# Delta rule: the next head's decay products between the halves of the first doubling, its sums of squares in four parts ahead of turns 1 to 4

## The reference, cut to what matters

```python
def chunked_gated_delta(q, k, v, g, beta):
    b = jnp.cumsum(g, axis=-1)
    diff = b[..., :, None] - b[..., None, :]
    dec = jnp.where(incl, jnp.exp(jnp.where(incl, diff, 0.0)), 0.0)
    k_beta = k * beta[..., None]
    A = jnp.where(strict, jnp.einsum('nbhid,nbhjd->nbhij', k_beta, k) * dec, 0.0)
    lhs = A + jnp.eye(C, dtype=A.dtype)
    ...
    sol = lax.linalg.triangular_solve(lhs, rhs, left_side=True, lower=True, unit_diagonal=True)
    ...
def deltanet_branch(q, k, v, z, a, bgate, conv_w, a_log, dt_bias, norm_g):
    qkv = jax.nn.silu(depthwise_conv(jnp.concatenate([q, k, v], -1), conv_w))
    q = l2norm(q.reshape(B, L, DN_HEADS, DN_DK)) * (DN_DK ** -0.5)
    k = l2norm(k.reshape(B, L, DN_HEADS, DN_DK))
```

## Time and profile before

| | us |
|---|---|
| timed runs | 2511.9, 2514.2, 2514.21 (median 2514.2) |
| the profiled execution | 2511.17 |
| its span | 2509.4 |
| TensorE busy in the span | 2391.3 (95%), 14993 matmuls |
| VectorE busy | 1712.1 (68%) |
| ScalarE busy | 1020.1 (41%) |
| GpSimd busy | 946.7 (38%) |

### The profile page before, as it was taken

The page is one execution under the profiler, slowest core; times in us unless marked ns, Lnnn a source line. Parts: engine busy times, 40 slices in busy tenths (PEclk is TensorE's granted clock), DMA queues, the critical chain, the costliest instruction groups (busy, mean ns, idle before and its releaser), DMA issues. The chain is left out here.

```text
span 2509.4 us, 44836 instructions
## 1 busy us (share of the span) xinstructions
PE 2391.3 (95%) x14993; PEld 1448.8 (58%) x14993; DVE 1712.1 (68%) x3600; ACT 1020.1 (41%) x1767; POOL 946.7 (38%) x612
## 2 busy tenths in 40 slices
PE   7999998989999999988999999998999999999998
PEld 6444444458878888875465556564656544444443
DVE  7535432037777677763260778998999689998887
ACT  4322332224433344322322344335989634443331
POOL 4421422412331223311522477876767422222220
PEclk9999999999999999999999999999999999999999
DMA  5321322221110011002323378987999699999994
GB/s 205 107 68 34 101 67 70 71 74 35 34 33 8 25 33 33 8 0 68 101 85 118 119 265 283 306 297 250 358 380 396 211 381 389 389 389 368 349 357 155
DMA packets 174318, 440.40 MB, mean 175 GB/s; under 512 B 17408, under 2 KB 83584, under 8 KB 174096
## 3 DMA queue, kind: packets, MB, share of 16 engines
q1 hardware_dynamic: 132752, 288.20, 33.3%
q0 software_dynamic: 36864, 134.23, 14.9%
q10 hardware_dynamic: 4608, 16.78, 1.7%
HBM read 395.11 MB, written 44.04 MB: 175 GB/s over the span
## 5 line engine op out<-in xcount | busy, mean ns | idle before, releaser
L2049 POOL TENSOR_TENSOR hid_u_lo<-hid_u,hid_u_hi 128x1024 bf16<-128x1024 f32 x128 | 290.7, 2272 | 168.4 <-ACT hid_u_hi L2033 159.5
L150 PE MATMUL bank<-hT_hi,hid_u_hi 128*128 128x384 bf16 x1024 | 335.2, 327 | 17.0 <-POOL hid_u_lo L2049 7.4
L150 PE MATMUL bank<-hT_hi,hid_u_lo 128*128 128x384 bf16 x1024 | 335.0, 327 | 0.0
L150 PE MATMUL bank<-hT_lo,hid_u_hi 128*128 128x384 bf16 x1024 | 335.0, 327 | 0.0
L214 POOL TENSOR_TENSOR w_shared_lo<-w_raw,w_shared_hi 128x1024 bf16<-128x1024 f32 x72 | 158.4, 2218 | 392.8 <-ACT w_shared_hi L209 392.8
L2033 ACT ACTIVATE hid_u_hi<-hid_u 128x1024 bf16<-128x1024 f32 x128 | 135.1, 1056 | 210.1 <-PE bank L150 145.8
L150 PE MATMUL bank<-hT_hi,w_shared_hi 128*128 128x264 bf16 (+2 forms) x704 | 202.6, 296 | 8.5 <-ACT dn_conv_in L1423 4.5
L150 PE MATMUL bank<-hT_lo,w_shared_hi 128*128 128x264 bf16 (+2 forms) x704 | 202.4, 296 | 0.0
L150 PE MATMUL bank<-hT_hi,w_shared_lo 128*128 128x264 bf16 (+2 forms) x704 | 202.4, 296 | 0.0
L150 PEld LDWEIGHTS bank<-hT_hi,hid_u_hi 128*128 128x128 bf16 x1024 | 100.4, 98 | 87.7 <-issue 22.3
L2740 PE MATMUL bank<-w_shared_hi,ex_gated_hi 128*128 128x512 bf16 x384 | 146.8, 382 | 4.0 <-DVE ex_gated_lo L2822 4.0
(11 more groups left out here) (513 smaller groups left out, 5840.9 us busy)
## 6 DMA issues: line engine op xcount, KB each, us to landing
hid_u<-in_peer_u SPq DMA_DIRECT2D x128, 512.0 KB
ex_v<-in_peer_v SPq DMA_DIRECT2D x128, 512.0 KB
w_raw<-in_w_ret SPq DMA_DIRECT2D x60, 512.0 KB, 4.2
expert_hidden<-hid_gelu SPq DMA_DIRECT2D x128, 192.0 KB
ex_gated<-expert_hidden SPq DMA_DIRECT2D x128, 192.0 KB
w_raw<-in_w_dn SPq DMA_DIRECT2D x32, 512.0 KB, 3.5
expert_weights<-ex_grid ACTq DMA_DIRECT2D x32, 512.0 KB
ex_weights<-expert_weights SPq DMA_DIRECT2D x64, 256.0 KB
```

The lines of the kernel that those rows point to most:

```text
L150: last = nc.tensor.matmul(out, left[l], right[r], start=start and i == 0, stop=stop and i == len(PASSES) - 1)
L2049: self.nc.gpsimd.tensor_tensor(self.us[1][:, m % 2, :, :], self.u32[:, m % RING, :, :], self.us[0][:, m % 2, :, :], ALU.subtract).then_inc ...
```

## The change

TensorE's order is changed, and the helpers are split so that the parts can be named. The other engines' orders stay. The list of parts ahead of the loop still has DECAYS and the whole SUMS.

```diff
-        pe_order = ("PROJ_Q PROJ_K turn0 PROJ_V grow1 DECAYS turn1 grow2 turn2 grow3 turn3 SUMS grow4 turn4 grow5 "
+        pe_order = ("PROJ_Q PROJ_K turn0 PROJ_V double1 DECAYS add1 SUMS.0 turn1 grow2 SUMS.1 turn2 grow3 SUMS.2 "
+                    "turn3 grow4 SUMS.3 turn4 grow5 "
...
-                    elif part == "SUMS":
-
-                        pe.wait_ge(s["sq_ready"], 2 * hn + 2)
-                        early.wait_free(pe, "ss", hn)
-                        for i in range(2):
-                            for t in range(NT + i):
...
-                        early.fills("ss", last)
+                    elif part.startswith("SUMS"):
+
+                        columns = [(i, t) for i in range(2) for t in range(NT + i)]
+                        mine = {"SUMS": slice(0, 9), "SUMS.0": slice(0, 2), "SUMS.1": slice(2, 4),
+                                "SUMS.2": slice(4, 6), "SUMS.3": slice(6, 9)}[part]
+                        if mine.start == 0:
+                            pe.wait_ge(s["sq_ready"], 2 * hn + 2)
+                            early.wait_free(pe, "ss", hn)
+                        for i, t in columns[mine]:
...
+                        if mine.stop == len(columns):
+                            early.fills("ss", last)
...
-                def grow(level, h):
+                def grow(level, h, first=True, second=True):
...
-                    if level:
+                    if first:
...
+                    if second:
...
+                    elif part.startswith("double"):
+                        grow(int(part[-1]), h, second=False)
+                    elif part.startswith("add"):
+                        grow(int(part[-1]), h, first=False)
```

More of the change, by code:

```diff
@@ L1268, in following @@
                                                            start=True, stop=True))
-                    elif part == "SUMS":
-                        pe.wait_ge(s["sq_ready"], 2 * hn + 2)
-                        early.wait_free(pe, "ss", hn)
-                        for i in range(2):
-                            for t in range(NT + i):
-                                last = nc.tensor.matmul(out("ss")[0:rows(t), NC5 * i + t:NC5 * i + t + 1],
-                                                        sq_meta[:, :] if t == NT else sq[:, i, t, :],
-                                                        ones[:, 0:1], start=True, stop=True)
-                        early.fills("ss", last)
+                    elif part.startswith("SUMS"):
[6 more added lines that the diff above has]
+                        for i, t in columns[mine]:
+                            last = nc.tensor.matmul(out("ss")[0:rows(t), NC5 * i + t:NC5 * i + t + 1],
+                                                    sq_meta[:, :] if t == NT else sq[:, i, t, :],
+                                                    ones[:, 0:1], start=True, stop=True)
+                        if mine.stop == len(columns):
+                            early.fills("ss", last)
                     elif part == "SCALES":
```

## The result

The changed kernel takes 2545.5 us (median of six runs, 2536.4 to 2548.7) against 2511.7 (six runs, 2509.6 to 2514.2) for the kernel before: a ratio of 1.0133, 95% interval 1.012 to 1.0146. It is 33.8 us slower. The forecast was slower, at 2527, with a range to 2536: the direction held, the size did not. Counted as a change, it was +12.9 us in the forecast, whose base of three runs lies 2.5 us higher, and is +33.8.

A forecast was written before the change was run, and what follows sets the result against it. The prediction took the level ring across TensorE, VectorE and ScalarE as the bound, not TensorE's busy time. Order and lockout, 7 x 1.73 = 12.1 us, plus net clock 0.8 gave 12.9; 2514.2 + 12.9 = 2527 us, range 2511 to 2536.

The forecast's parts named there:

- What bounds the stretch: Head loop: each level's chain across TensorE, VectorE and ScalarE sets the pace, not TensorE's 95% busy share.
- The ring: One level's cycle: first half, VectorE masks, second half, VectorE subtraction, transposes, ScalarE copies; 5.45 us in level 4.
- DECAYS, 0.76 late: Level 1: decay products of 1.94 us in a 1.03 us hole start the second half 0.76 us later.
- The lockout: Level 2: GpSimd's second and third weight subtractions block v's convolution taps on VectorE; second half 2.14 us later.
- Rival 2: Level 2: v's taps take as long as before, only shifted; 2.5 us less 4.2 of clock, 2513; 18%.
- Sums ahead of the turns, 0.44 each exposed, 1.4 given back at level 4: Turns 2 to 4: SUMS.1 adds 0.39 us, the removed whole SUMS returns 1.38, SUMS.3 adds 0.58.
- 12.1 us for all this: Head loop: order and lockout leave each of seven passes 1.73 us late, 12.1 us in all.
- The granted clock, net +0.8: Head loop: new half-clock stretches in four of seven passes cost 5.0 us, less 4.2 us for the old ones.
- the old falls: Half-clock stretches behind the whole SUMS in three of seven passes, 1.4 us each, 4.2 us, expected to vanish.
- the hole: Level 2: TensorE's new wait between first and second half, forecast at 3.5 us.
- rival 3: Level 2's hole costs the clock in every pass: 12.1 + 9.8 - 4.2 = 17.7 us, 2532; 12%.
- Rival 1: Moved decay products and sums fill TensorE's waits: about 17 us gained and 4.2 of clock, 2493; 10%.

The follow-up runs named there:

- e5: Kernel before, with the nine sums split between the halves of levels 1 and 2 and between forward and backward transposes of turns 2 and 3: 2498.0 us, ratio 0.9952.
- e9: Against e5: ScalarE's SPLIT_K and SPLIT_V later, no sums between level 2's halves, two each inside turns 2, 3 and 4: 2495.1 us, ratio 0.9927.
- e3: Changed kernel with ScalarE's SPLIT_V moved behind turn 3, so GpSimd's third weight subtraction comes later: 2507.3 us, ratio 0.9981 to the kernel before.
- e2: Kernel before with only the sums moved, in four parts ahead of turns 1 to 4, decay products left behind level 1: 2505.3 us, ratio 0.9971.
- e4: Changed kernel plus twelve matmuls a pass, read by nobody, between the halves of level 2: 2519.1 us, ratio 1.0029 to the kernel before.
- e7: Changed kernel with SUMS.1 moved from ahead of turn 2 to ahead of turn 3, beside SUMS.2: 2528.1 us, ratio 1.0071 to the kernel before.
- e8: Changed kernel plus four matmuls a pass, read by nobody, between the halves of level 2: 2526.5 us, ratio 1.0064 to the kernel before.

## Why the prediction was right and wrong

*What bounds the stretch*: right. The ring of first half, masks, second half, subtraction, turn sets the pace, and TensorE's 95% said nothing. e5 and e9 place 1.9 us a pass of TensorE work inside the ring's gaps at no cost.

*DECAYS, 0.76 late*: right, 3.86 for 3.11 us.

*The lockout*: right in its sequence, in its instants (the first tap 6.62 us and the third subtraction 9.14 us behind level 1's start, 6.62 and 9.13 forecast) and nearly in size: level 2's second half 1.98 us late for 2.14 forecast, taps of 2.10, 0.77, 2.51. e3 removes the third subtraction's part of it by moving that subtraction. Rival 2, no new lockout, is out.

*Sums ahead of the turns, 0.44 each exposed, 1.4 given back at level 4*: right, with 0.2 less given back (6.08 us and not 5.93 between the second halves of levels 3 and 4, in the changed kernel as in e2 and e5). e2 was expected at 2504.5 from these terms and the removed falls, and measured 2505.3.

*12.1 us for all this*: 11.7 by e4. Up to here the mechanism and the size were right, and not by luck: each term has a row of its own.

*The granted clock, net +0.8*: this step failed, the new falls at "four of seven and somewhat less than the full price, 5.0 us", and with it its bounds, 0 to 9.8. The runs showed 26.4 us in its place. The 7.5 us that are left of the 33.8 are 11.7 for the order less 4.2 for the old falls. The count was too low, seven passes and not four, but that alone would have been 9.8 us; that the hole might bring the clock down in every pass was seen (rival 3, 2532). What was mis-sized is the price of a fall: 3.8 us a pass and not 1.4. I took 1.4 us from a fall of 3.4 us behind the sums, the only kind in the loop's rows, and multiplied. The new falls are of 10 us.

Nothing in the rows of the head loop showed a longer one. The same trace had it just behind the loop, in TensorE's wait of 8.0 us before the last head and beyond it, and the bound left it out (the first row is TensorE's timeline, the second the busy times of a stretch, with the granted clock of 0.50 behind GpSimd's):

```profile
1112.29 1.97 PE L1329 MATMUL bank<-ident,dn_xt 128*128 128x128 f32 x8 [8.01 <-DVE dn_x_meta L1677]
```

```profile
1106.50:1116.70 10.20, 4.41 (x21) 4.33 (x22) 5.25 (x6) 4.71 (x7) 6.03 (x6) 0.50 0.00 0
```

An estimate from it: a fall of 10.24 us costs at most half its length, 5.1 us, or 36 in seven passes. With that as its upper end the range would have held the result. e7 shows that the length is not the hole's alone: with SUMS.1 a level later it is 3.4 us in six of the seven passes and the price some 9 us instead of 26 (2528.1 less 2519.1).

*Rival 1, the holes fill*: out for the change as it is; the same idea with each piece no longer than its hole, and beside the ring instead of ahead of it, gives e5.

## What to carry to other kernels

Where two engines lock each other out, work out for each instant who is issued first: a delay of under 1 us on a third engine turned the order round here, and two of three taps were held up by over 1 us each where one was. Compare the length of what is moved with the hole it is to fill, and ask which operation behind it the next stage waits for; a piece between the forward and the backward half was free where the same piece ahead of both was not. And bound the price of a new idle stretch on TensorE by the longest slow stretch that the trace shows anywhere, not by the nearest.

## What the runs showed of the hardware that was not expected

Matmuls that compute nothing of use made the kernel faster: twelve a pass in the hole, 26.4 us. The hole alone does not set what a fall costs: a wait of 3.1 us cost 3.8 us in falls each pass in the changed kernel and 1.3 in e7, with the same wait and other work behind it. A wait of 2.2 us (e8) brought the clock down in three of seven passes, one of 1.5 us (e3) in none. And TensorE need not be idle: in the kernel before, the clock fell behind the nine sums in three of seven passes, though it had worked on them without a wait; with the sums in parts (e2) it did not.
